# Constants and the first normalisation in one block, with plain transposes of scaled tiles and half a projection unit inside

## The chip, the cores and the metric

The kernel runs on one core of one Trainium2 chip. The metric is the device time of the program in microseconds (us), the median of the runs of a kernel. The engines are TensorE (PE, with its weight loads as PEld), VectorE (DVE), ScalarE (ACT), GpSimd (POOL) and SyncE (SP), whose queue issues every DMA here. They run side by side and wait for each other by semaphores.

## The reference

A two-layer decoder trunk on x (1, 1024, 1024) float32. Each layer is an RMS norm, one input projection, a token mixer, a gate, an output projection and a residual add. Layer 0 is a gated DeltaNet with 8 heads in chunks, layer 1 a dilated sliding-window attention with three groups of 8 heads. What matters here:

```
def rms_norm(x, g):
    y = x * lax.rsqrt(jnp.mean(x * x, axis=-1, keepdims=True) + EPS)
    return y * g
for i in range(2):
    h = rms_norm(x, norm_g[i])
    y = mixer_i(h, ...)          # proj = h @ w_in; layer 0 takes 16 columns of it as b_logit, a_logit
    x = x + y
```

In layer 0 the 16 logit columns give beta (a sigmoid) and g (the log decay of each step and head); the decays are summed along the positions before any head can use them.

## The kernel before, in words

The program is a row of blocks, and a block ends on all engines before the next begins: constants, the first norm (n0), the DeltaNet heads, the output projection (p0), the second norm (n1), the attention heads, the output projection (p1). Loads into SBUF and matmuls of a block wait for its begin.

**Constants** (lines 82 to 188). SP loads seven small tensors. POOL makes the identity and masks one after the other (line 124), PE turns the loaded rows into columns (lines 163 to 171), DVE copies them out of PSUM (lines 183 to 188), and POOL cuts the last mask behind that.

**norm_and_turn** (line 230) makes from x, 8 tiles of 128 tokens, the transposed normalised activations in two parts: g.h_hi, rounded to the matmul format fp32r, and g.h_lo, the rest. Tile t: ACT squares it with a running sum (line 270), takes Ln (272) and Exp (274), which gives 1/rms; DVE scales the identity by it into diag (301); PE multiplies 8 blocks of x by diag (289), which turns and scales at once, and each of these float32 matmuls is two passes in the trace; DVE multiplies by the gain into hf (307); ACT copies hf into h_hi (279); DVE subtracts into h_lo (313). ACT works on tile t and on the copy of tile t-2 by turns. x comes in four loads (tiles 0, 1, 2 to 4, 5 to 7; line 260), the first projection weights behind them (line 211), and these are split into parts the same way (221, 226) at the end of the stage.

**delta_heads** (line 340). PE first projects the 16 logit columns for all 1024 tokens: 2 halves of 24 matmuls of 128x512 (three_passes, line 336, in thirds of 8). ACT evacuates the halves (591), PE transposes them (713), ACT and DVE make beta and the log decay (593 to 601, 888 to 895), PE sums them with two matmuls (718, 719), ACT and DVE finish the columns (603 to 605, 900 to 905), POOL picks head 0's part (545, 548). Then comes an order written out by hand: 36 slots a head on PE, in each a third (8 matmuls) of a projection unit of the next head, and behind it the small matmuls of the current one; 3 slots make one half of a unit. The other engines follow the same slots: the evacuation of a half (658), the convolution (981, 983), the weight splits (585, 876).

SP's queue is in order: a wait in it holds all later loads.

## Time and profile before

| | us |
|---|---|
| median of 3 runs | 2462.3 (2461.72 to 2463.55) |
| profiled execution: span of the core, first to last instruction | 2456.9 |
| median minus span (start and end of the program around it) | 5.4 |
| PE, DVE, ACT, POOL busy | 2336.6, 1439.4, 1263.6, 232.5 |
| n0 ends (last h_lo), first logit matmul | 40.36, 40.67 |
| first matmul of head 0 | 58.42 |
| n1 ends (last h_lo), first attention matmul | 1219.75, 1220.07 |

The profile is of one execution; the page gives no time of its own for it beside the span. All times in the rows are from the span's start. A float32 matmul or a weight load has a modelled end, so the distance from one start to the next is the better measure of PE's pace. A granted clock of 1.00 is 2.4 GHz and 0.50 is 1.2 GHz; before its first change in the trace the clock is written as 1.00 whatever it was. "Idle before" a row is the time its engine stood still, with what ended it.

### The profile page before, as it was taken

The numbers are of one execution on the slowest core, as the hardware profiler recorded it, in microseconds if no ns is written. First come the engines' busy times: TensorE is split into PE (matmuls) and PEld (weight loads), VectorE is DVE, ScalarE is ACT, GpSimd is POOL, SyncE is SP. The second block draws the span as 40 slices with busy tenths as digits, with TensorE's granted clock in tenths as the row PEclk, the third lists the DMA queues.
The fourth block names the chain that finished last, engine by engine and source line by source line (L and its number), as shares of the span: only waits on it lengthen the run. The fifth ranks groups of instructions, "written<-read, shape, count | busy, mean of one in ns | idle before, by whom it ended". The sixth has DMA issues, their size and how long they took to land. (4 is left out here: it accounts for less than half of the span.)

```text
span 2456.9 us, 35479 instructions
## 1 busy us (share of the span) xinstructions
PE 2336.6 (95%) x11486; PEld 1941.4 (79%) x11486; DVE 1439.4 (59%) x2646; ACT 1263.6 (51%) x2564; POOL 232.5 (9%) x387
## 2 busy tenths in 40 slices
PE   6999999999999998799699999999999999999969
PEld 5778887887878786588688888888888888888757
DVE  4746666575757573676473655738284654738255
ACT  4546555565655554454554545455454545454433
POOL 1021221202020202640000000000000000000000
PEclk9999999999999998899899999999999999999979
DMA  3021222203021211688411211121121211121167
GB/s 114 28 62 49 52 53 59 74 27 84 27 72 29 71 40 33 216 278 264 178 35 36 61 40 47 33 60 35 41 63 35 60 35 47 39 56 38 18 230 267
DMA packets 280352, 189.41 MB, mean 77 GB/s; under 512 B 72173, under 2 KB 258693, under 8 KB 280229
## 3 DMA queue, kind: packets, MB, share of 16 engines
q1 hardware_dynamic: 280228, 187.88, 25.8%
q8 instruction: 64, 1.05, 0.2%
q14 instruction: 60, 0.48, 0.1%
HBM read 160.38 MB, written 27.46 MB: 76 GB/s over the span
## 5 line engine op out<-in xcount | busy, mean ns | idle before, releaser
L336 PE MATMUL b_proj<-g_h_hi,wb_w_hi 128*128 128x512 f32 x1280 | 510.7, 399 | 5.0 <-PEq L234 5.0
L336 PE MATMUL b_proj<-g_h_hi,wb_w_lo 128*128 128x512 f32 x1280 | 511.2, 399 | 0.0
L336 PE MATMUL b_proj<-g_h_lo,wb_w_hi 128*128 128x512 f32 x1280 | 510.2, 399 | 0.0
L336 PE MATMUL a_proj<-g_h_hi,wa_w_hi 128*128 128x512 f32 x784 | 324.2, 414 | 7.0 <-PEq L234 6.1
L336 PE MATMUL a_proj<-g_h_lo,wa_w_hi 128*128 128x512 f32 x784 | 323.4, 413 | 0.0
L336 PE MATMUL a_proj<-g_h_hi,wa_w_lo 128*128 128x512 f32 x784 | 317.4, 405 | 0.0
L336 PEld LDWEIGHTS b_proj<-g_h_hi,wb_w_hi 128*128 128x128 f32 x1280 | 241.4, 189 | 53.9 <-issue 5.2
L336 PEld LDWEIGHTS b_proj<-g_h_hi,wb_w_lo 128*128 128x128 f32 x1280 | 241.2, 188 | 50.0
L336 PEld LDWEIGHTS b_proj<-g_h_lo,wb_w_hi 128*128 128x128 f32 x1280 | 241.4, 189 | 49.2
L1536 ACT ACTIVATE b_acc<-b_proj,g_gains 128x512 f32<-128x512 f32 x96 | 66.1, 688 | 294.6 <-DVE b_qk L1792 208.2
L336 PEld LDWEIGHTS a_proj<-g_h_hi,wa_w_hi 128*128 128x128 f32 x784 | 149.0, 190 | 38.0 <-issue 8.7
L1689 DVE TENSOR_TENSOR wb_w_lo<-wb_raw,wb_w_hi 128x1024 fp32r<-128x1024 f32 x79 | 95.9, 1214 | 139.7 <-ACT wb_w_hi L1497 139.7
L1158 PE MATMUL p_y<-p_w_hi,p_a_hi 128*128 128x512 f32 x384 | 152.2, 396 | 26.6 <-DVE p_w_lo L1125 26.6
L336 PEld LDWEIGHTS a_proj<-g_h_lo,wa_w_hi 128*128 128x128 f32 x784 | 148.9, 190 | 30.6 <-issue 1.0
L336 PEld LDWEIGHTS a_proj<-g_h_hi,wa_w_lo 128*128 128x128 f32 x784 | 149.0, 190 | 28.7
L1158 PE MATMUL p_y<-p_w_lo,p_a_hi 128*128 128x512 f32 x384 | 151.4, 394 | 0.0
L1158 PE MATMUL p_y<-p_w_hi,p_a_lo 128*128 128x512 f32 x384 | 151.1, 394 | 0.0
L983 DVE SCALAR_TENSOR_TENSOR a_acc<-a_x_raw,a_hw,a_acc 128x512 f32<-128x512 f32 x192 | 144.3, 751 | 6.8
L1125 DVE TENSOR_TENSOR p_w_lo<-p_w_raw,p_w_hi 128x1024 fp32r<-128x1024 f32 x96 | 126.8, 1321 | 0.0
L1757 DVE TENSOR_TENSOR b_sq_lo<-b_sg,b_sq_hi 128x512 fp32r<-128x512 f32 x96 | 66.2, 689 | 84.9 <-ACT b_sq_hi L1541 84.9
L1113 ACT ACTIVATE p_a_hi<-p_a_raw 128x256 fp32r<-128x256 f32 x96 | 40.1, 418 | 145.5 <-PE p_y L1158 87.6
L1158 PEld LDWEIGHTS p_y<-p_w_hi,p_a_hi 128*128 128x128 f32 x384 | 73.3, 191 | 43.3 <-DVE p_w_lo L1125 28.0
(229 smaller groups left out, 4230.7 us busy)
## 6 DMA issues: line engine op xcount, KB each, us to landing
wb_raw<-in_b_w_in_dram SPq DMA_DIRECT2D x80, 512.0 KB, 3.9
p_w_raw<-in_a_w_out_dram SPq DMA_DIRECT2D x64, 512.0 KB, 3.9
wa_raw<-in_a_w_in_dram SPq DMA_DIRECT2D x48, 512.0 KB, 4.2
p_w_raw<-in_b_w_out_dram SPq DMA_DIRECT2D x32, 512.0 KB, 4.1
a_out<-a_og SPq DMA_DIRECT2D x64, 128.0 KB, 1.8
p_a_raw<-a_out SPq DMA_DIRECT2D x64, 128.0 KB, 4.8
a_zx<-inverse_tiles SPq DMA_DIRECT2D x16, 384.0 KB, 4.4
u_tiles<-a_u SPq DMA_DIRECT2D x8, 512.0 KB, 3.2
```

The source lines that it names most:

```text
L336: last = pe.matmul(out, w[:, k, :], a[:, k, ks], start=(n == 0), stop=(n == 23))
L983: ins = dve.scalar_tensor_tensor(acc[:, half], src, w, acc[:, half], ALU.mult, ALU.add)
L1113: act.activation(a_hi[c][:, :], a_raw[:, c, :], ACT.Copy).then_inc(high, 1)
L1125: dve.tensor_tensor(w_lo[c][:, :], w_raw[:, c, :], w_hi[c][:, :].bitcast(F32), ALU.subtract).then_inc(low, 1)
L1158: mm = pe.matmul(y[part % 2][b][:, :], a_[c][:, ts], w_[c][:, ns], start=(first and c == 0 and n == 0), stop=(last and c == RING - 1 and n ...
L1536: act.activation(acc[:, half], proj[half][:, :], ACT.Copy, scale=r.gains[:, gain:gain + 1]).then_inc(rope, 1)
L1689: dve.tensor_tensor(w_lo[slot_of(j)][:, :, :], raw[:, slot_of(j)], w_hi[slot_of(j)][:, :, :].bitcast(F32), ALU.subtract).then_inc(w_low, 1)
L1757: dve.tensor_tensor(sq_lo[:, :], sg[:, q % 2], sq_hi[:, :].bitcast(F32), ALU.subtract).then_inc(sq_low, 1)
```

## The change

There is no block of its own for the constants. They become a class whose parts are issued inside the block of the first norm stage: the small loads behind x tile 0 on SP, the masks on POOL, the turns first on PE, the rows and copies first on DVE. Their PSUM space is the second projection bank, which is now allocated ahead of the block. In both norm stages the weight row of the norm is loaded to all 128 partitions (a broadcast of 4 KB to 512 KB, between x tile 0 and tile 1), and DVE makes xs = x * (1/rms) * row in one scalar_tensor_tensor per tile; PE turns xs by plain transposes with the identity (one pass each, 8 a tile); h_hi and h_lo are made straight from PSUM. diag, hf and the gain multiply are gone, and the ring has 3 tiles instead of 4. The split of the first weights comes at tile 5 instead of at the end. In the first stage PE works off the first half unit of the logits (tokens 0 to 511) in thirds behind the transposes of tiles 5, 6 and 7. In delta_heads only the second half is left in front, and the two decay matmuls move from before the first head to its slot 2.

```diff
-def constants(nc, g, norm_g, a_norm_g, b_q_norm_g, b_k_norm_g, a_conv_w, a_log, a_dt_bias):
-
-    with ExitStack() as ctx:
...
-        ps = m.ps("ps", [P, 512])
+class Constants:
...
+    def allocate(self, ctx):
+        m = Mem(self.nc, ctx, "c")
...
+    def load(self, sp):
+        rows, landed = self.rows, self.landed
+        sp.dma_start(rows[0:16, :], self.norm_g.rearrange("l (k c) -> (l k) c", c=P)).then_inc(landed, 16)
+        sp.dma_start(rows[16:18, :], self.a_norm_g.rearrange("l (k c) -> (l k) c", c=P)).then_inc(landed, 16)
+        sp.dma_start(rows[18:21, :], self.b_q_norm_g.rearrange("l g c -> (l g) c")).then_inc(landed, 16)
+        sp.dma_start(rows[21:24, :], self.b_k_norm_g.rearrange("l g c -> (l g) c")).then_inc(landed, 16)
+
+        sp.dma_start(self.conv_rows[:, :], self.a_conv_w.rearrange("l j (c n) -> (l j c) n", n=P)).then_inc(landed, 16)
+        sp.dma_start(self.head_row[:, 0:H], self.a_log).then_inc(landed, 16)
+        sp.dma_start(self.head_row[:, H:2 * H], self.a_dt_bias).then_inc(landed, 16)
...
+    def split_high(self, act, slot):
+        act.wait_ge(self.landed[slot], 16)
+        act.activation(self.hi[slot][:, :, :], self.raw[:, slot], ACT.Copy).then_inc(self.high, 1)
+
+    def split_low(self, dve, slot):
+        dve.wait_ge(self.high, slot + 1)
+        dve.tensor_tensor(self.lo[slot][:, :, :], self.raw[:, slot], self.hi[slot][:, :, :].bitcast(F32),
+                          ALU.subtract).then_inc(self.low, 1)
+
+
+def norm_and_turn(nc, tag, g, src, norm_g, layer, weights, constants=None, logits=None):
+
+
+    RING = 3
+    EARLY = T // 2 + 1
+        gain = m.sb("gain", [P, D])
         stat = m.sb("stat", [P, T, 3])
-        diag = m.sb("diag", [P, RING, P])
-        hf = m.sb("hf", [P, RING, KD, P])
+        xs = m.sb("xs", [P, RING, D])
         turned_ps = m.ps("turned_ps", [P, RING, KD, P])
+        if constants:
+            constants.allocate(ctx)
...
             for i, (a, b) in enumerate(loads):
                 sp.dma_start(x[:, a:b, :], src[a * P:b * P, :].rearrange("(t p) n -> p t n", p=P)
                              ).then_inc(landed[i], 16)
+                if i == 0:
+                    if constants:
+                        constants.load(sp)
+                    sp.dma_start(gain[:, :], norm_g[layer:layer + 1, :].partition_broadcast(P)
+                                 ).then_inc(gain_landed, 16)
             weights.load(sp)
+
+        if constants:
+            @block.gpsimd
+            def _(pool):
+                constants.masks(pool)
...
-                if t == T:
-                    weights.split_high(act)
                 if t >= 2:
-                    act.wait_ge(gained, t - 1)
-                    act.activation(g.h_hi[:, :, tokens(t - 2)], hf[:, (t - 2) % RING], ACT.Copy).then_inc(high, 1)
+                    act.wait_ge(turned, t - 1)
+                    act.activation(g.h_hi[:, :, tokens(t - 2)], turned_ps[:, (t - 2) % RING], ACT.Copy).then_inc(high, 1)
+                if t == EARLY:
+                    weights.split_high(act, 0)
+                if t == T and weights.split_both:
+                    weights.split_high(act, 1)
 
         @block.tensor
         def _(pe):
+            if constants:
+                constants.turn(pe)
             for t in range(T):
-                pe.wait_ge(landed[load_of[t]], 16)
-                pe.wait_ge(scales, t + 1)
+                pe.wait_ge(scaled, t + 1)
                 if t >= RING:
-                    pe.wait_ge(gained, t - RING + 1)
+                    pe.wait_ge(low, t - RING + 1)
                 for k in range(KD):
-                    last = pe.matmul(turned_ps[:, t % RING, k, :], x[:, t, k * P:(k + 1) * P], diag[:, t % RING, :],
-                                     start=True, stop=True)
+                    last = pe.transpose(turned_ps[:, t % RING, k, :], xs[:, t % RING, k * P:(k + 1) * P], g.ident[:, :])
                 last.then_inc(turned, 1)
+                third = t - EARLY
+                if logits is not None and third >= 0:
+                    if third == 0:
+                        pe.wait_ge(low, TH)
+                        pe.wait_ge(weights.low, 1)
+                    three_passes(pe, logits, weights.hi[0], weights.lo[0], g.h_hi, g.h_lo, slice(0, HALF), third)

         @block.vector
         def _(dve):
+            if constants:
+                constants.make_rows(dve)
             weights.clear(dve)
+            if constants:
+                constants.keep(dve)
+            dve.wait_ge(gain_landed, 16)
             for t in range(T + 2):
                 if t < T:
                     dve.wait_ge(stats, 3 * t + 3)
                     if t >= RING:
                         dve.wait_ge(turned, t - RING + 1)
-                    dve.tensor_scalar(diag[:, t % RING, :], g.ident[:, :], stat[:, t, 2:3], None,
-                                      ALU.mult).then_inc(scales, 1)
-                if 1 <= t <= T:
-                    dve.wait_ge(turned, t)
-                    if t > RING:
-                        dve.wait_ge(low, t - RING)
-                    dve.tensor_tensor(hf[:, (t - 1) % RING], turned_ps[:, (t - 1) % RING], spread(gain, 2, P),
-                                      ALU.mult).then_inc(gained, 1)
-                if t == T + 1:
-                    weights.split_low(dve)
+                    dve.scalar_tensor_tensor(xs[:, t % RING, :], x[:, t, :], stat[:, t, 2:3], gain[:, :],
+                                             ALU.mult, ALU.mult).then_inc(scaled, 1)
                 if t >= 2:
                     dve.wait_ge(high, t - 1)
-                    dve.tensor_tensor(g.h_lo[:, :, tokens(t - 2)], hf[:, (t - 2) % RING],
+                    dve.tensor_tensor(g.h_lo[:, :, tokens(t - 2)], turned_ps[:, (t - 2) % RING],
                                       g.h_hi[:, :, tokens(t - 2)].bitcast(F32), ALU.subtract).then_inc(low, 1)
+                if t == EARLY:
+                    weights.split_low(dve, 0)
+                if t == T and weights.split_both:
+                    weights.split_low(dve, 1)
...
+SETUP_DECAYS = 2
...
-def delta_heads(nc, g, weights, o_turned):
+def delta_heads(nc, g, weights, proj, o_turned):
...
-        proj = [m_.ps(f"proj{i}", [P, HALF]) for i in range(2)]
...
+            pe.sem_inc(proj_mm, 1)
             pe.wait_ge(w_low, 1)
-            for b in range(2):
-                for third in range(3):
-                    last = three_passes(pe, proj[b][:, :], w_hi[0], w_lo[0], g.h_hi, g.h_lo,
-                                        slice(b * HALF, (b + 1) * HALF), third)
-                last.then_inc(proj_mm, 1)
+            for third in range(3):
+                last = three_passes(pe, proj[1][:, :], w_hi[0], w_lo[0], g.h_hi, g.h_lo, slice(HALF, S), third)
+            last.then_inc(proj_mm, 1)
 
             pe.wait_ge(evac, 2)
             for t in range(T):
                 last = pe.transpose(turn[:, t * 2 * H:(t + 1) * 2 * H], ba[:, t * P:(t + 1) * P],
                                     g.ident[0:2 * H, 0:2 * H])
             last.then_inc(setup, 1)
-            pe.wait_ge(setup, 12)
-            log = cols[:, C_LOG].rearrange("p t h -> p (t h)")
-            pe.matmul(turn[:, 256:256 + T * H], g.tri[:, :], log, start=True, stop=True)
-            pe.matmul(turn[:, 384:384 + T * H], g.ones[:, :], log, start=True, stop=True).then_inc(setup, 1)
+
+            def decays():
+                pe.wait_ge(setup, 12)
+                log = cols[:, C_LOG].rearrange("p t h -> p (t h)")
+                pe.matmul(turn[:, 256:256 + T * H], g.tri[:, :], log, start=True, stop=True)
+                pe.matmul(turn[:, 384:384 + T * H], g.ones[:, :], log, start=True, stop=True).then_inc(setup, 1)
...
                 for s in range(SLOTS):
+                    if m is None and s == SETUP_DECAYS:
+                        decays()
...
-        constants(nc, g, norm_g, a_norm_g, b_q_norm_g, b_k_norm_g, a_conv_w, a_log, a_dt_bias)
...
             weights = WeightSlots(nc, layer, "wa", a_w_in[0], first, True)
-            norm_and_turn(nc, "n0", g, x[0], 0, weights)
-            delta_heads(nc, g, weights, a_out)
+            proj = [Mem(nc, layer, "a").ps(f"proj{i}", [P, HALF]) for i in range(2)]
+            constants = Constants(nc, g, proj[1], norm_g, a_norm_g, b_q_norm_g, b_k_norm_g, a_conv_w, a_log, a_dt_bias)
+            norm_and_turn(nc, "n0", g, x[0], norm_g, 0, weights, constants, proj[0][:, :])
+            delta_heads(nc, g, weights, proj, a_out)
...
-            norm_and_turn(nc, "n1", g, x1, 1, weights)
+            norm_and_turn(nc, "n1", g, x1, norm_g, 1, weights)
...
```

The parts of Constants that are left out (masks, turn, make_rows, keep) hold the same instructions as the old block. Left out as well: the renamed semaphores.

## Rows read from the trace of the kernel before

**Rows 1.** First part of the page: busy time, share of the span, instructions.

```profile
PE 2336.6 (95%) x11486; PEld 1941.4 (79%) x11486; DVE 1439.4 (59%) x2646; ACT 1263.6 (51%) x2564; POOL 232.5 (9%) x387
```

**Rows 2.** Busy time by window: length, engines in order, granted clock, DMA share, GB/s.

```profile
12.00:14.00 2.00, 0.00 (x0) 0.00 (x0) 0.00 (x0) 1.59 (x5) 0.00 (x0) 1.00 1.01 412
...
42.00:44.00 2.00, 2.00 (x6) 1.52 (x5) 0.00 (x0) 0.00 (x0) 0.44 (x1) 0.50 0.30 88
...
40.67:58.42 17.75, 14.71 (x60) 11.63 (x61) 1.14 (x6) 3.73 (x10) 1.77 (x1) 0.87 0.41 118
...
70.00:600.00 530.00, 518.04 (x2613) 428.14 (x2612) 337.65 (x602) 302.52 (x626) 90.69 (x205) 1.00 0.20 52
...
1183.57:1220.07 36.50, 17.90 (x129) 16.96 (x129) 23.77 (x29) 21.96 (x43) 0.00 (x0) 0.81 0.48 173
```

**Rows 3.** Timeline, start: start, duration, engine, line, what [idle before <-releaser].

```profile
8.71 1.83 SPq L260 DMA_DIRECT2D n_x<-in_x_dram  x4
...
12.35 1.06 ACT L270 ACTIVATE n_sq<-n_x 128x1024 f32<-128x1024 f32 x1 [2.35 <-DMA n_x<-in_x_dram]
...
14.44 7.48 PE L289 MATMUL n_turned_ps<-n_diag,n_x 128*128 128x128 f32 x48 [8.99 <-DVE n_diag L301]
...
17.81 1.06 ACT L270 ACTIVATE n_sq<-n_x 128x1024 f32<-128x1024 f32 x1 [2.33 <-DMA n_x<-in_x_dram]
```

**Rows 4.** Timeline of the first norm stage in its steady part.

```profile
22.90 1.04 ACT L270 ACTIVATE n_sq<-n_x 128x1024 f32<-128x1024 f32 x1
...
24.41 1.04 ACT L279 ACTIVATE g_h_hi<-n_hf 128x1024 fp32r<-128x1024 f32 x1
...
24.95 1.22 DVE L307 TENSOR_TENSOR n_hf<-n_turned_ps,g_gains 128x1024 f32<-128x1024 f32 x1
...
25.36 1.04 ACT L270 ACTIVATE n_sq<-n_x 128x1024 f32<-128x1024 f32 x1
```

**Rows 5.** Timeline from the end of that stage to the head's slot 2, TensorE.

```profile
39.14 1.22 DVE L313 TENSOR_TENSOR g_h_lo<-n_hf,g_h_hi 128x1024 fp32r<-128x1024 f32 x1
...
40.67 0.77 PE L336 MATMUL a_proj<-g_h_hi,wa_w_hi 128*128 128x512 f32 x1 [6.13 <-PEq L234]
...
45.45 0.40 PE L336 MATMUL a_proj<-g_h_hi,wa_w_lo 128*128 128x512 f32 x1
...
53.85 0.39 PE L336 MATMUL a_proj<-g_h_hi,wa_w_lo 128*128 128x512 f32 x1
...
54.92 0.67 PE L713 MATMUL a_turn<-g_ident,a_acc 16*128 16x16 f32 x8 [0.68 <-ACT a_acc L591]
...
57.95 0.43 PE L718 MATMUL a_turn<-a_cols,g_tri 128*128 128x64 f32 x2 [2.36 <-DVE a_cols L895]
...
58.42 0.48 PE L336 MATMUL a_proj<-g_h_hi,wa_w_hi 128*128 128x512 f32 x1
...
62.62 0.40 PE L336 MATMUL a_proj<-g_h_hi,wa_w_lo 128*128 128x512 f32 x1
...
63.77 0.39 PE L336 MATMUL a_proj<-g_h_lo,wa_w_hi 128*128 128x512 f32 x1
```

**Rows 6.** DMA: landing time of line 1481's loads; issues of x up to 70 us.

```profile
DMA to landing us min/median/max: 3.4/3.9/4.2
...
n_x<-in_x_dram SPq DMA_DIRECT2D x2, 1536.0 KB, 10.0
```

**Rows 7.** Timeline of TensorE round a head's transposes; then a group of the page.

```profile
104.70 0.60 PE L814 MATMUL a_turn<-g_ident,a_acc 128*128 128x128 f32 x4
...
105.06 0.48 PE L336 MATMUL a_proj<-g_h_hi,wa_w_hi 128*128 128x512 f32 x1
...
L983 DVE SCALAR_TENSOR_TENSOR a_acc<-a_x_raw,a_hw,a_acc 128x512 f32<-128x512 f32 x192 | 144.3, 751 | 6.8
```

**Rows 8.** Timeline of the second norm stage (ScalarE) and behind it (TensorE).

```profile
1198.10 1.06 ACT L270 ACTIVATE n_sq<-n_x 128x1024 f32<-128x1024 f32 x1 [2.31 <-DMA n_x<-x]
...
1220.07 0.77 PE L336 MATMUL b_proj<-g_h_hi,wb_w_hi 128*128 128x512 f32 x1 [5.00 <-PEq L234]
```

182 lines of the change are left out of this document (83 added, 99 removed).

## The prediction

> **What bounds the kernel now.** I read the page's busy shares first: TensorE (PE) is busy 95% of a span of 2456.9 us, VectorE (DVE) and ScalarE (ACT) 59% and 51% [rows 1]. So a change pays only where PE stands still or runs at its lower clock, and the next view to read is the busy time by stretch. In the 17.75 us after the first norm stage PE is busy 14.71 us at a mean clock of 0.87; in the second norm stage it is busy 17.90 us of 36.50 [rows 2]. These edges are what the change touches. Everything between them is dense PE work with nothing in it changed, so I take it that it only slides: what is won before the first head is won at the end.
>
> The timeline of the start shows the first edge. The block of constants comes first and x is loaded only behind it, at 8.71; its first tile is squared at 12.35 (3.64 us later), and ACT begins tile 2 at 17.81, when the third load has landed [rows 3]. From there the stage runs in a fixed beat: ACT squares a tile, takes Ln and Exp, copies an older tile into h_hi, and squares the next, 22.90 to 25.36, 2.46 us a tile with no gap; DVE is as full, with diag, the gain multiply (1.22) and h_lo (1.22) [rows 4, 5]. PE has room: a tile's sixteen passes take it 2.02 us. The stage ends with the last h_lo, 39.14 + 1.22 = 40.36, and PE starts the projection of the head logits at 40.67 [rows 5].
>
> That projection is 48 matmuls. Up to 45.45 they start every 0.43 us (11 of them), then every 0.233 us (the last at 53.85) [rows 5]. The windows give the slow part a clock of 0.50, that is 1.2 GHz [rows 2], after PE had stood idle for 6.13 us; the fast part has 2.4 GHz. Then come the small transposes (54.92), an idle time of 2.36 us while ACT and DVE make the decays, two small matmuls at 57.95, and the first head's first matmul at 58.42. It is slow again: 11 matmuls up to 62.62 take 4.20 us where 11 x 0.233 = 2.56 would do. The 17th, which begins slot 2, starts at 63.77 [rows 5]. I use this event as the mark: what happens up to it is changed, from it on the program is the same.
>
> **The change, part by part.** (1) One block for constants and norm. x tile 0 is issued at 0.83 instead of 8.71. Seven small loads and the broadcast norm row stand before the rest of x on SP's queue. The small ones took 0.83 to about 3.4 to issue; behind tile 0 they end near 3.7, so the broadcast goes out at 3.7 and x tile 1 at 4.2. A broadcast of this very shape (one row to 128 partitions, 512 KB) lands 3.4 to 4.2 us after issue [rows 6], here at about 7.4. Once it flows, x comes in at 412 GB/s [rows 2], 1.3 us for half a megabyte and 3.8 for the three tiles of a 1536 KB load, which before landed some 10 us after its issue because it queued behind the others [rows 6]. Queued behind the broadcast, tile 1 lands near 8.7 and tiles 2 to 4 at about 12.5. I take 12.6 for the start of tile 2 on ACT, 5.2 us earlier than 17.81: 7.9 us of earlier issue, less 1.4 for the small loads' issue and 1.3 for half a megabyte more. Bounds 11.5 and 14.5 (the broadcast overlapping fully, or the small loads delaying it). The constants themselves are covered: PE's turns and DVE's five copies, done at 6.2 before, are done at about 7, and DVE's first scaling waits for the broadcast, 7.4, in any case; POOL's masks are beside it.
>
> (2) The new tile. DVE loses diag and the PSUM multiply and gains one scalar_tensor_tensor of 128x1024. There is none in the trace; the 128x512 one takes 751 ns [rows 7], a tensor_tensor of 1024 takes 1.22 [rows 4], so it lies between 1.2 and 1.5; I take 1.25, since most of an instruction's time is per element. DVE then needs 2.4 a tile, ACT still 0.95 + 0.22 + 0.24 + 0.10 + 0.95 = 2.46. ACT's h_hi copy now reads PSUM; a 128x512 copy from PSUM takes 0.59, no more than SBUF ones, so nothing is added. The beat stays 2.46: the removed DVE work is worth nothing by itself. PE's sixteen passes become eight transposes: four take 0.36 us at the full clock in a head (104.70 to 105.06) [rows 7], so 0.72 and some 0.25 to drain; at the half clock twice that, at most 0.23 each as the first tiles' passes show (48 in 7.48 us, 1.9 us over the later rate) [rows 3]. Either is under 2.46.
>
> (3) Where this puts the tail. From 12.6: tile 5's square starts at 12.6 + 3 x 2.46 = 20.0; its h_hi companion ends at 22.5; the weight split of slot 0 on ACT 23.45, on DVE 25.1 (weights landed near 17). So the first third of the logits' half unit starts at 25.15, right behind tile 5's transposes. Now PE is in series with the tiles: third 0, tile 6, third 1, tile 7, third 2. A third is 8 matmuls: 3.4 us slow, 1.87 fast. I assume the clock rises during or just after third 0, as it did after 2.5 to 4.8 us of PE work at 14.44, 40.67 and 58.42: third 0 ends at 28.55, tile 6 at 30.0, third 1 at 31.9, tile 7 at 32.8, third 2 at 34.7. h_hi of tile 7 ends at 33.9, its h_lo at 35.1. Block end 35.1, next matmul 35.4 (the 0.31 us step of [rows 5]).
>
> (4) After the stage. Only 24 logit matmuls are left. PE has been idle under 1 us before them, so I take them at 0.233: 5.6 us. Last result to transposes 0.83 + 0.55 as before, then slots 0 and 1 of the head (16 x 0.23 = 3.7) at once, which more than covers the 2.36 us that the decays need, then the two decay matmuls 0.47. Mark at 35.4 + 5.6 + 1.38 + 3.7 + 0.47 = 46.55 against 63.77: 17.2 us earlier. By parts: 5.3 for the stage, 5.6 for the half unit that moved into it, 2.4 idle, 2.2 and 1.65 for the two slow starts of the clock. A cost hides here: the decays' last exponentials, the head's taps and the weight split of unit 1 were done before slot 2 began and now come after it. ACT is through them 2.45 us after the mark, DVE 3.7, so the first convolution begins about 0.9 us later than it did; the second one waits for its own half's evacuation, so this is absorbed, and PE's next weights are due only 4 slots (7.4 us) after the mark. If that cover were gone, the price would be this 0.9 us once.
>
> (5) The second norm stage has the same new tiles and no constants. The broadcast stands between tile 0 and tile 1 there, and tile 2 on ACT already waits for its load (1198.10) [rows 8], so the beat starts 1.3 us later. The weight split moved from the tail into it (0.95 on ACT, which is now full to the end: last Exp at 1199.4 + 5 x 2.46 + 0.94 + 1.6 = 1214.25), but the tail is shorter: scaling 1.25, transposes 1.0 to 1.8, h_hi 1.05, h_lo 1.2. End 1218.9 to 1219.7 against 1219.75. PE's start there was slow before too (1220.07, idle 5.00 us) [rows 8]. I take zero; bounds -1 and +2 (the clock's slow start longer by half, or the broadcast costing more).
>
> The Trainium skill, "TensorE: Matmul & The Clock Gate", Part 4: PE-mode transpose, speaks against the change: the full clock does not engage for transposes, which do not count as PE work the way matmuls do. The trace of before has 128-wide transposes only in fours between dense matmuls at the full clock [rows 7], so it neither confirms nor denies it. By it, taking matmuls out of the norm stage takes the warming out too, which is the first rival below.
>
> **Sum.** Own time of the profiled execution: span 2456.9; the median of the runs is 2462.3, 5.4 more lies around the span and is not touched. 2456.9 - 17.2 + 0 = 2439.7 span, 2445.1 us.
>
> **Rivals.** A, slow tail: transposes and short thirds leave PE at 1.2 GHz to the end of the stage and through the half unit. Third 0 to 28.55, tile 6 30.0, third 1 33.4, tile 7 34.9, third 2 38.3; block end 38.7, matmuls from 39.0, 24 of them at the pace of [rows 5] 7.8: mark 52.35, 11.4 saved, 2450.9. For it: five tiles of transposes at 40% of the beat or less before third 0. Against: third 0 alone is 3.4 us of dense matmuls, about what raised the clock at 58.42. B, fast tail: the clock is at 2.4 GHz from tile 2 on, as it was with the matmuls. Third 0 ends at 27.0, last h_lo at 32.9, mark 44.35: 19.4 saved, 2442.9. C, the saving does not survive: the first head's chain (setup, convolution, block inverses and their round trip through memory) sets the pace of the first heads, not PE, and it starts hardly earlier than PE's cover shrinks, or the new loads crowd the start; under 4.9 us left, 2457.4 to 2467. Against: from 70 to 600 PE is busy 518.04 of 530 us [rows 2]. D, slower: DVE's wait for the broadcast stands at the head of its queue in both stages; behind it is every scaling, transposes and h_hi. It decides against the change if the 128 reads of one row take over 17 us more together than the 4 us of [rows 6], say 10 us each: 2462.3 + 3 = 2465. Against: the row of that shape, measured eight times.
>
> **How the numbers follow.** Forecast 0.57, A 0.20, B 0.15, C 0.05, D 0.03. Prediction 2445.1. The range takes in B with a second stage at -1, 2442, and A with +2, 2453. Under 0.2% (4.9 us) a measurement of this kernel can hardly be told from no change, so: faster 0.92, same 0.05, slower 0.03.
>
> **What would show it.** Right: x issued at 0.8; tile 2's square near 12.6; a beat of 2.46 on ACT with DVE below it; 8 transposes a tile; third 0 at 25; a projection start near 35.4 with PE idle under 1 us before; no idle between the logits' transposes and the head; the mark near 46.5, and the same distance from mark to end except for the second norm stage. Wrong: a clock of 0.50 between 30 and 45 (A); tile 2's square after 14.5; gaps in PE in the first head that were not there (C); a second stage over 2 us longer.

## The result, and the profile after

Median 2449.4 us (2446.8 to 2450.2, four runs) against 2462.0 (2458.5 to 2463.6, four runs): ratio 0.9946, interval 0.9932 to 0.996. The change saves 12.6 us; 17.2 were forecast. The time lies inside the range, 4.3 us above the forecast and close to rival A's 2450.9, though mostly not for A's reason. The profiled execution has a span of 2445.1 and took 2446.8. From the page after, its first part:

```profile
PE 2324.5 (95%) x11358; PEld 1927.6 (79%) x11358; DVE 1438.4 (59%) x2630; ACT 1262.9 (52%) x2564; POOL 230.8 (9%) x387
```

TensorE's busy time fell by 12.1 us against [rows 1] and the span by 11.8. No share tells what happened; the edges do. The timeline of after, from the start to the first third of the half unit (start, duration, engine, line, what [idle before <-releaser]):

```profile
0.83 0.39 SPq L269 DMA_DIRECT2D n_x<-in_x_dram  x1
...
3.73 0.35 SPq L274 DMA_DIRECT2D n_gain<-in_norm_g_dram  x1
...
8.12 1.28 DVE L333 SCALAR_TENSOR_TENSOR n_xs<-n_x,n_stat,n_gain 128x1024 f32<-128x1024 f32 x1 [0.90 <-DMA n_gain<-in_norm_g_dram]
...
13.32 1.06 ACT L289 ACTIVATE n_sq<-n_x 128x1024 f32<-128x1024 f32 x1 [2.26 <-DMA n_x<-in_x_dram]
...
18.16 1.05 ACT L289 ACTIVATE n_sq<-n_x 128x1024 f32<-128x1024 f32 x1
...
18.73 1.97 PE L311 MATMUL n_turned_ps<-g_ident,n_xs 128*128 128x128 f32 x8 [0.45 <-DVE n_xs L333]
...
20.58 1.05 ACT L289 ACTIVATE n_sq<-n_x 128x1024 f32<-128x1024 f32 x1
21.14 1.64 PE L311 MATMUL n_turned_ps<-g_ident,n_xs 128*128 128x128 f32 x8 [0.45 <-DVE n_xs L333]
...
23.56 1.09 PE L311 MATMUL n_turned_ps<-g_ident,n_xs 128*128 128x128 f32 x8 [0.78 <-DVE n_xs L333]
...
25.92 0.76 PE L365 MATMUL a_proj<-g_h_hi,wa_w_hi 128*128 128x512 f32 x1 [1.26 <-DVE wa_w_lo L233]
...
29.04 0.43 PE L365 MATMUL a_proj<-g_h_lo,wa_w_hi 128*128 128x512 f32 x1
...
30.10 0.47 PE L365 MATMUL a_proj<-g_h_hi,wa_w_lo 128*128 128x512 f32 x1
...
35.94 0.47 PE L365 MATMUL a_proj<-g_h_hi,wa_w_hi 128*128 128x512 f32 x1 [1.05 <-PEq L242]
...
42.37 0.66 PE L740 MATMUL a_turn<-g_ident,a_acc 16*128 16x16 f32 x8 [0.68 <-ACT a_acc L619]
...
46.75 0.33 PE L747 MATMUL a_turn<-a_cols,g_tri 128*128 128x64 f32 x2
...
47.11 0.48 PE L365 MATMUL a_proj<-g_h_lo,wa_w_hi 128*128 128x512 f32 x1
```

x is issued at 0.83, tile 2 is squared at 13.32 in place of 17.81 ([rows 3]), and the beat is 2.42 us (18.16 to 20.58). The projection behind the stage starts at 35.94 (40.67 before), at full pace; nothing waits between the small transposes and the head (2.36 us in [rows 5]); the mark, last row, is at 47.11 against 63.77.

The windows of after round third 0 and in the second norm stage (length, PE, PEld, DVE, ACT, POOL, granted clock, DMA share, GB/s):

```profile
24.00:26.00 2.00, 0.74 (x7) 0.53 (x5) 2.00 (x3) 1.94 (x6) 0.00 (x0) 0.93 0.00 0
26.00:28.00 2.00, 2.00 (x5) 1.61 (x6) 2.00 (x2) 1.94 (x6) 0.00 (x0) 0.50 0.00 0
28.00:30.00 2.00, 2.00 (x11) 1.62 (x11) 2.00 (x3) 0.88 (x1) 0.00 (x0) 0.72 0.00 0
...
1190.00:1193.00 3.00, 2.55 (x12) 2.15 (x12) 3.00 (x3) 2.88 (x9) 0.00 (x0) 0.50 0.09 23
1193.00:1195.00 2.00, 1.21 (x11) 0.97 (x10) 2.00 (x3) 2.00 (x3) 0.00 (x0) 0.98 0.00 0
...
1197.00:1203.00 6.00, 3.94 (x16) 3.14 (x16) 5.35 (x5) 4.48 (x8) 0.00 (x0) 0.50 0.00 0
1205.00:1209.00 4.00, 4.00 (x10) 3.13 (x11) 1.22 (x1) 2.04 (x2) 0.00 (x0) 0.50 0.45 131
```

The last four windows are the second norm stage and the attention matmuls behind it. The timeline of after there:

```profile
1172.87 0.32 SPq L269 DMA_DIRECT2D n_x<-x  x1
...
1177.70 1.06 ACT L289 ACTIVATE n_sq<-n_x 128x1024 f32<-128x1024 f32 x1 [3.54 <-DMA n_x<-x]
...
1184.10 1.06 ACT L289 ACTIVATE n_sq<-n_x 128x1024 f32<-128x1024 f32 x1 [2.22 <-DMA n_x<-x]
...
1203.20 1.23 DVE L337 TENSOR_TENSOR g_h_lo<-n_turned_ps,g_h_hi 128x1024 fp32r<-128x1024 f32 x1 [0.85 <-ACT g_h_hi L296]
...
1204.74 0.76 PE L365 MATMUL b_proj<-g_h_hi,wb_w_hi 128*128 128x512 f32 x1 [2.64 <-PEq L242]
...
1210.00 0.47 PE L365 MATMUL b_proj<-g_h_hi,wb_w_hi 128*128 128x512 f32 x1
```

Twelve times the next matmul starts 0.43 us or more behind the last before the pace becomes 0.23 (1210.00); before the change it was six times. So the first edge came out as forecast and the second did not.

The distances between the same events in several profiles, in us (the names of the other kernels are explained below), show where the 17.2 went. "First layer out" is the output projection of layer 0, "tile 2's square" is ScalarE's first work on tile 2 of the second norm stage, and slow matmuls are the first ones of the attention projection whose successor starts over 0.4 us later:

| stretch | before | before_again | after | after_again | n1_old | gain_early | warm |
|---|---|---|---|---|---|---|---|
| start to mark | 63.77 | 63.75 | 47.11 | 47.45 | 47.44 | 45.59 | 45.63 |
| mark to last projection matmul of layer 0 (the heads) | 869.72 | 868.48 | 872.36 | 871.54 | 872.31 | 873.99 | 873.14 |
| mark to last first-layer-out matmul | 1119.30 | 1119.21 | 1119.65 | 1120.63 | 1119.87 | 1123.56 | 1120.93 |
| last first-layer-out matmul to tile 2's square | 15.03 | 15.19 | 17.34 | 17.22 | 16.03 | 15.94 | 17.24 |
| tile 2's square to first attention matmul | 21.96 | 21.92 | 20.64 | 20.64 | 21.37 | 20.54 | 19.77 |
| slow matmuls there | 6 | 7 | 12 | 11 | 6 | 8 | 0 |
| first to last attention projection matmul (with its slow start) | 1104.70 | 1106.43 | 1106.80 | 1106.66 | 1105.49 | 1106.10 | 1103.88 |
| last of these to first matmul of the second output projection | 36.76 | 37.84 | 37.37 | 37.28 | 35.30 | 35.27 | 37.72 |
| last matmul to end | 6.13 | 6.14 | 7.07 | 7.07 | 6.12 | 7.07 | 6.13 |

In spans: 16.66 won at the mark; 1.0 lost in the second stage (+2.31 to tile 2, -1.32 behind it); 1.2 lost to the longer slow start (six more slow matmuls at 0.20 each); 0.94 lost at the last store; 11.8 left, so 1.7 are in the long stretches between. The two profiles of the unchanged kernel differ by 1.7 and 1.1 in two such stretches, and by 3.2 in span: the net 1.7 can't be told from the spread of one execution.

Inside it is something that can. The heads of layer 0, whose code behind the mark is the same, took 868.5 to 869.7 us in the three profiles with the old order in front of them (before, before_again and one_block, explained below) and 871.3 to 876.1 in all eleven others; both kinds were profiled on two of the chips, and the gap is there on each. In after they are 2.6 us longer, and a stretch behind them, up to the end of the output projection, that came out 2.3 us shorter hides it. PE's waits in the heads, first in before (63.77 to 933.4), then in after (47.11 to 919.5), with total, times and longest in us:

```profile
PE a_first L858 <- DMA a_zx<-inverse_tiles: 4.2, 4, 3.2
...
PE a_first L889 <- DMA a_zx<-inverse_tiles: 6.7, 6, 3.6
```

2.5 us more wait for the block inverses that come back through memory, which is the chain that rival C named. What in the change lengthens it was not tested; decays_front and logits_back, which undo a part each, have it too (872.3 and 876.1).

### The profile page after: what moved, and what is told of

Same layout as the page of the kernel before. It is cut to its first block and busy times, and to the rows that moved or that the text cites. A ratio compares the mean times of both kernels' runs of the same rounds, so it can differ in the third digit from the quotient of the medians.

```text
span 2445.1 us, 35190 instructions
## 1 busy us (share of the span) xinstructions
PE 2324.5 (95%) x11358; PEld 1927.6 (79%) x11358; DVE 1438.4 (59%) x2630; ACT 1262.9 (52%) x2564; POOL 230.8 (9%) x387
```

## The experiments

Each is an edit of the changed kernel unless it says so; kernels in one group ran on one chip with the same runs of before, so medians of different groups are best compared by their ratio to before.

**The two kernels again (before_again, after_again).**

> The kernel before, unchanged, to learn how far one execution differs from another. In the profile of the changed kernel the head's slot 2 began 16.7 us earlier than before, but the span was only 11.8 us shorter; 4.9 us went between slot 2 and the end. Theory 1 (the loss is the change's own, at the second norm stage): this second profile of before repeats the first within 0.5 us in every stage, above all 929.7 us from slot 2 (63.77) to the last transposed output of the heads (993.50) and 1104.7 us from the first to the last attention projection matmul. Theory 2 (the loss is the spread of single executions): these stages differ by 1 to 2 us between the two profiles of the same code.

> The changed kernel, unchanged, timed in five rounds. Theory 1: median 12 to 13 us below before again, and in the profile the second norm stage with the slow start of the attention behind it costs the same 2 to 3 us more than before. Theory 2: a saving of 15 to 17 us in these rounds, the first result having been a low draw.

Measured: before_again 2462.5 us, ratio 1.0003 (0.9994 to 1.0012); after_again 2448.3, 0.9945 (0.9931 to 0.9958). The saving is 13.8 and 12.6 in two comparisons. before_again's profile differs from before's by 1.7 us in the attention projection, so its Theory 2 (the spread of single executions) holds for the long stretches; after_again's Theory 1 holds for the median and for the second stage and the end, whose distances repeat to 0.2 us in these pairs.

**Second norm stage as before (n1_old).** The first stage is the changed one, the second runs the old method.

```diff
-            norm_and_turn(nc, "n1", g, x1, norm_g, 1, weights)
+            norm_and_turn_old(nc, "n1", g, x1, 1, weights)
```

> The changed kernel with the second norm stage as it was before (matmuls with the scaled identity, gain multiply, no broadcast); the first stage stays changed. In the changed kernel the 13 first attention matmuls ran at the half clock (7 before), and the third x load of that stage was squared 6.4 us after the first (5.7 before). Theory 1: 2 to 3 us faster than the changed kernel (slow start back to 7 matmuls, 1.2 us; last tile's turn 0.9; load 0.7 to 1.3), the first attention matmul about 1 us earlier after the last matmul of the output projection, 37.0 us instead of 38.0. Theory 2 and the forecast of zero for this stage: no difference beyond 1 us.

Measured: 2446.4 us, 0.9941 (0.9928 to 0.9955), 1.9 better than after_again in the medians. From last layer-out matmul to first attention matmul it takes 37.40 against 37.86, it has 6 slow matmuls in place of 11, and its last store lands 0.95 sooner. These are the three losses of the table, taken back in part: 0.5, 1.0 and 0.95. The intervals overlap; the profile's distances carry the reading, and they are one execution's. In this pair the new method costs about 1.5 us in the second stage and is worth nothing there. But the old method does not always do better: one_block, which has it too, takes 38.30 us for the same stretch and has 12 slow matmuls behind it, with the same idle time of 5.00 us as before. Timeline of one_block:

```profile
1215.28 0.77 PE L362 MATMUL b_proj<-g_h_hi,wb_w_hi 128*128 128x512 f32 x1 [5.00 <-PEq L243]
...
1220.53 0.44 PE L362 MATMUL b_proj<-g_h_hi,wb_w_hi 128*128 128x512 f32 x1
```

There the granted clock was full from 1193.3 and fell at 1213.8, 1.5 us before the projection; in before it fell at 1219.6, 0.5 us before it. So the slow start was 6, 7, 6 and 12 matmuls with the old method, and 11 to 13 in six profiles with the new one (8 in gain_early).

**PE kept at its full clock (warm).** Matmuls of a constant, whose results nobody uses, fill PE's gaps in both stages.

```diff
+            def keep_warm(n):
+                for _ in range(n):
+                    pe.matmul(idle[:, :], g.ones_r[:, :], warm[:, :], start=True, stop=True)
...
+            keep_warm(10 if constants else 16)
             for t in range(T):
...
+                if t < 5 if constants else t < 7:
+                    keep_warm(3)
+                elif not constants:
+                    keep_warm(8)
```

> The changed kernel with matmuls of constants added on TensorE in its idle time in both norm stages (10 and 16 before the first tile, 3 behind each of tiles 0 to 4 and 0 to 6, 8 behind tile 7 of the second stage); their results go to a spare bank and are not used. Theory 1 (plain transposes do not keep TensorE at the full clock, and this costs at the stage ends): the windows show 1.00 from the first tiles on, third 0 of the half unit takes 1.9 us instead of 3.4, a tile's turn 1.1 instead of 2.0, the attention starts with no slow matmul; first logit matmul behind the stage near 34.3 instead of 35.9, in all 4 to 6 us faster than the changed kernel. Theory 2 (the clock is not what costs): the same time within 1 us.

Measured: 2444.5 us, 0.9931 (0.9917 to 0.9944), 3.8 below after_again; the intervals overlap a little. Timeline of warm, TensorE:

```profile
23.65 1.09 PE L322 MATMUL n_turned_ps<-g_ident,n_xs 128*128 128x128 f32 x8 [0.63 <-DVE n_xs L349]
26.01 0.47 PE L381 MATMUL a_proj<-g_h_hi,wa_w_hi 128*128 128x512 f32 x1 [1.26 <-DVE wa_w_lo L233]
...
34.46 0.47 PE L381 MATMUL a_proj<-g_h_hi,wa_w_hi 128*128 128x512 f32 x1 [0.96 <-PEq L242]
...
1203.57 0.47 PE L381 MATMUL b_proj<-g_h_hi,wb_w_hi 128*128 128x512 f32 x1 [0.79 <-PEq L242]
```

Third 0 runs at full pace from its first matmul, the stage ends 1.5 us sooner (34.46), and the attention projection has no slow start. So the clock was worth 1.5 to 1.8 us at the first edge and, at the second, 0.87 in the stage's tail (20.64 to 19.77) and some 2.3 in the start behind it (11 or 12 x 0.2). The last store lands 0.95 sooner here too; it did so in n1_old as well, where the clock is not held. That is 5.8 against a difference of 5.3 in the spans and 3.8 in the medians.

**The second stage turned by matmuls (n1_matmul_turn).** The data and the order stay; each transpose becomes a float32 matmul with the identity, which is two passes, so PE also gets twice the passes.

```diff
-                    last = pe.transpose(turned_ps[:, t % RING, k, :], xs[:, t % RING, k * P:(k + 1) * P], g.ident[:, :])
+                    if constants:
+                        last = pe.transpose(turned_ps[:, t % RING, k, :], xs[:, t % RING, k * P:(k + 1) * P], g.ident[:, :])
+                    else:
+                        last = pe.matmul(turned_ps[:, t % RING, k, :], xs[:, t % RING, k * P:(k + 1) * P], g.ident[:, :],
+                                         start=True, stop=True)
```

(constants are given in the first stage alone)

> The changed kernel with the turns of the second stage made by float32 matmuls with the identity (two passes, 16 a tile) instead of plain transposes; all else equal. Theory (matmul passes raise the clock, transposes hardly do): the windows of that stage show 1.00 from the second or third tile on as before the change, a tile's turn 2.0 us, the attention starts with 7 or fewer slow matmuls instead of 13 (1.2 us less), the stage's own length stays. Median 0.5 to 1.5 us below the changed kernel. Rival: the clock follows the share of time in which TensorE is busy, whatever it does; then the same share of passes at 2.0 us in a beat of 2.41 gives the same half clock, and nothing changes.

Measured: 2446.2 us, 0.9932 (0.9919 to 0.9944; its highest run 2451.7), beside 0.9945 (0.9931 to 0.9958) for the changed kernel: the intervals overlap, and the profiled execution is the slowest of the six, so again the reading rests on the stage in one profile. Windows and timeline of n1_matmul_turn:

```profile
1190.00:1192.00 2.00, 2.00 (x12) 2.00 (x12) 0.77 (x1) 1.94 (x5) 0.00 (x0) 0.54 1.01 406
1192.00:1194.00 2.00, 2.00 (x18) 1.90 (x18) 2.00 (x3) 1.94 (x6) 0.00 (x0) 1.00 1.11 321
```

```profile
1203.28 2.05 PE L314 MATMUL n_turned_ps<-g_ident,n_xs 128*128 128x128 f32 x16 [1.41 <-DVE n_xs L337]
...
1210.30 0.47 PE L369 MATMUL b_proj<-g_h_hi,wb_w_hi 128*128 128x512 f32 x1 [2.64 <-PEq L242]
```

Sixteen passes a tile at 2.05 us in place of eight transposes at 1.97, so the stage is as long (20.72 from tile 2). But the clock rises at 1191.8, in the second tile, and stays, and the projection starts at full pace behind the same idle time of 2.64 us. In the changed kernel, behind the same idle time, the clock was already low. So in this pair what PE did in the stage, and not the idle gap behind it, decided the twelve slow matmuls. Whether the kind of instruction counts or its amount is not shown: before the clock rises a tile's sixteen passes keep PE busy for 3.6 us, without a gap, and eight transposes for 1.97 of 2.42 us. The forecast's rival (the share of busy time decides) is not excluded by this test, and pad_b below speaks for it.

**Parts undone: the decays in front (decays_front), the half unit behind the stage (logits_back).**

```diff
+            decays()
+
             def body(m, n, p):
...
-                    if m is None and s == SETUP_DECAYS:
-                        decays()
```

> The changed kernel with the two decay matmuls back in front of the first head, as before. Theory (each part pays at its own place and keeps it): TensorE idles again 2.3 us after the logits' transposes, and the clock falls for about 3.4 us of the first head's matmuls (1.65 us lost); the head's slot 2 begins 3.5 to 4.2 us later than in the changed kernel (47.1 to 47.5), and the median is 3 to 4.5 us above it, near 2452. Rival (what is won at the start is given back in the heads): slot 2 is later by the same, but the span and the median are not, within 1.5 us.

```diff
-            norm_and_turn(nc, "n0", g, x[0], norm_g, 0, weights, constants, proj[0][:, :])
+            norm_and_turn(nc, "n0", g, x[0], norm_g, 0, weights, constants)
```

(and all 48 logit matmuls behind the stage)

> The changed kernel without the half unit in the norm stage: both halves of the logits behind it, the decays still at slot 2. The stage should end 1.5 to 2.4 us earlier (no thirds between the transposes), the logits take 24 matmuls more and start at the half clock: first matmul behind the stage near 34, second half's end near 47.5 against 41.5. Theory: slot 2 of the head 5.5 to 6 us later than in the changed kernel, median near 2454. Rival (the half unit only moved, since it holds up the tiles): under 3 us.

Measured: decays_front 2453.8, 0.9965 (0.9952 to 0.9978), 5.5 above the changed kernel's 2448.3; logits_back 2454.8, 0.9967 (0.9955 to 0.998), 6.5 above. Their intervals meet its own (0.9931 to 0.9958) at the edge only. Timeline of decays_front, and of logits_back:

```profile
41.47 0.66 PE L740 MATMUL a_turn<-g_ident,a_acc 16*128 16x16 f32 x8 [0.68 <-ACT a_acc L619]
44.50 0.43 PE L747 MATMUL a_turn<-a_cols,g_tri 128*128 128x64 f32 x2 [2.36 <-DVE a_cols L926]
```

```profile
34.21 0.77 PE L365 MATMUL a_proj<-g_h_hi,wa_w_hi 128*128 128x512 f32 x1 [2.83 <-PEq L242]
48.74 0.67 PE L741 MATMUL a_turn<-g_ident,a_acc 16*128 16x16 f32 x8 [0.68 <-ACT a_acc L619]
```

The idle 2.36 us of [rows 5] is back to the hundredth, with the slow start behind it: mark 50.31, though its stage had happened to end 0.9 earlier (transposes 41.47 against 42.37), so 4.1 for the order alone. Without the thirds the stage ends 1.7 sooner (34.21) and the small transposes come 6.4 later (48.74): the 24 matmuls cost the stage 1.7 and save 8.1 behind it, which is their 5.6 and a slow start. The mark is at 53.50.

**Second norm row loaded early (gain_early).** The row of layer 1 is fetched in the output projection of layer 0.

```diff
-        gain = m.sb("gain", [P, D])
+        gain = m.sb("gain", [P, D]) if constants else g.gain1
...
+            if rope_tables:
+                sp.dma_start(rope_tables.g.gain1[:, :], rope_tables.norm_g[1:2, :].partition_broadcast(P)
+                             ).then_inc(rope_tables.g.gain1_landed, 16)
```

> The changed kernel with the second stage's weight row loaded at the end of the output projection before it, into a tile of its own. Theory (the 512 KB in the queue between tile 0 and tile 1 costs 1.3 to 2 us there): from the last matmul of the first output projection to the square of tile 2 15.1 to 15.5 us instead of 17.2 to 17.3, and the first attention matmul 1.3 to 2 us earlier; median 1 to 2 us below the changed kernel. Rival (those 2 us are the DMA's spread or the stores' landing): the distance stays above 16.5.

Measured: 2445.6 us, 0.9932 (0.9919 to 0.9945), 2.7 below the changed kernel's 2448.3, with overlapping intervals. The distance to tile 2 is 15.94 for 17.34, and 16.03 in warm_gain_early, which has the early row too; all eight profiles with the broadcast in the queue have 17.15 to 17.37. So the broadcast between x tile 0 and the rest costs 1.1 to 1.4, as step (5) had it. Its first edge was quick too (mark 45.59) though that code is the same. Timeline of gain_early, to be held against its three rows in after (21.14, 23.56, 25.92):

```profile
21.18 1.97 PE L311 MATMUL n_turned_ps<-g_ident,n_xs 128*128 128x128 f32 x8 [0.45 <-DVE n_xs L333]
23.60 1.83 PE L311 MATMUL n_turned_ps<-g_ident,n_xs 128*128 128x128 f32 x8 [0.45 <-DVE n_xs L333]
25.96 0.47 PE L365 MATMUL a_proj<-g_h_hi,wa_w_hi 128*128 128x512 f32 x1 [0.53 <-DVE wa_w_lo L233]
```

In after the full pace came on tile 4 (1.64), held for tile 5 (1.09) and was gone when third 0 began; here it came as tile 5 ended, and third 0 had all of it. So of this profile's gain 1.5 is the clock's phase at the first edge, and 1.3 is what the edit explains; how the 2.7 in the medians divides is not shown.

**Before with the constants' block alone (one_block).** An edit of the kernel before: one block, x issued first, a ring of 3 tiles, but the old scaling and the old turn by diag, and no broadcast.

```diff
-        constants(nc, g, norm_g, a_norm_g, b_q_norm_g, b_k_norm_g, a_conv_w, a_log, a_dt_bias)
...
+            proj = [Mem(nc, layer, "a").ps(f"proj{i}", [P, HALF]) for i in range(2)]
+            constants = Constants(nc, g, proj[1], norm_g, a_norm_g, b_q_norm_g, b_k_norm_g, a_conv_w, a_log, a_dt_bias)
+            norm_and_turn(nc, "n0", g, x[0], 0, weights, constants)
```

> The kernel before with one part of the change alone: the constants inside the block of the first norm stage (small loads behind x tile 0, masks, turns and copies there), the old tile method, ring of 3 tiles. Theory (the stage's gain is the earlier load, less 1.3 us for the broadcast that the whole change adds): tile 2 squared near 12.0 instead of 17.81, first logit matmul near 34.5 to 35 instead of 40.67, and the same 5.5 to 6 us at the end; median near 2456.5. Rival (the plain transposes and the fused scaling carry part of the stage's gain): under 4 us.

Measured: 2458.5 us, 0.9969 (0.996 to 0.9979), 8.1 less than the before of its comparison (2466.5; 5.2 to 9.9 by the interval, where 5.5 to 6 were expected). Timeline of one_block, TensorE:

```profile
34.40 0.77 PE L362 MATMUL a_proj<-g_h_hi,wa_w_hi 128*128 128x512 f32 x1 [6.13 <-PEq L243]
...
48.73 0.66 PE L738 MATMUL a_turn<-g_ident,a_acc 16*128 16x16 f32 x8 [0.68 <-ACT a_acc L616]
51.76 0.43 PE L743 MATMUL a_turn<-a_cols,g_tri 128*128 128x64 f32 x2 [2.37 <-DVE a_cols L920]
```

34.40 for 40.67: the early issue of x is worth 6.3 us; up to the mark the rest is as before (idle 6.13, idle 2.37), and the mark moves by 6.2. Tile 2 is squared at 11.42 here and at 13.32 in after, which also waits for the broadcast. Of the 16.66 at the mark the block gives 6.2, the half unit 6.4 (logits_back) and the later decays 4.1 (decays_front); by this sum the new tile, with its broadcast, is left with about nothing.

**Warm and early row together (warm_gain_early).**

> The changed kernel with both additions: matmuls of constants in TensorE's idle time of both norm stages, and the second stage's weight row loaded behind the output projection. If the two add up: 5 to 6 us below the changed kernel, median 2442 to 2443.5, faster than all others. Rival: the first attention matmul is bound by the beat of ScalarE, and the earlier load is worth nothing once the clock is up: 2444.5.

Measured: 2447.2 us where before takes 2466.5: 0.9922 (0.9909 to 0.9935), 19.3 us saved, the lowest ratio of all. The median itself missed the forecast 2442 to 2443.5, since this chip is some 4 us slower with before too. Against the change itself (0.9945, 0.9931 to 0.9958) the ratio is 0.23% of 2466 lower, 5.7 us, as forecast, but its interval meets that one at the edge and overlaps those of warm and gain_early. From the last layer-out matmul to the first attention matmul it takes 35.80 us, 37.01 in warm and 36.47 in gain_early, so the early row still pays 1.2 with the clock up, against the rival. The added matmuls did not hold the clock without fail: it fell for 3.4 us at 18.2 and again at 1188.9.

**A few tiny matmuls in the first block (pad_a 8, pad_b 20),** to move the later code in memory without touching the second stage.

```diff
                 constants.turn(pe)
+                pe.wait_ge(constants.kept, 5)
+                for _ in range(8):
+                    pe.matmul(constants.ps[:, 0:1], g.ones_r[:, :].bitcast(F32), g.ones[:, 0:1], start=True, stop=True)
```

> The changed kernel with 8 matmuls of one column added on TensorE in its idle time before the first tile (32 instructions with their weight loads; their result is not used), to move TensorE's code against the blocks in which code is fetched. In the changed kernel the last store landed 3.66 us after its issue in both executions (2.7 in the kernel before, n1_old and warm), with one packet of an instruction queue in that stretch, and the second stage's first x load 4.8 us after issue (3.2), with one or two such packets. Theory (fetched code shares the DMA engines with these loads, and where it falls hangs on the code's length): with the code shifted, at least one of the two landings goes back to 2.7 and 3.2, and its stretch has no packet of that queue. Rival (the landing times have another cause): both stay at 3.66 and 4.8 whatever the code.

> As pad_a with 20 such matmuls (80 instructions). Theory: a landing is long in the runs whose stretch holds a packet of an instruction queue and short in the others, in this run as in the rest. Rival: no such relation.

Measured, one execution each: 2449.8 and 2454.1 us. Against this chip's 2466.5 for before that is 16.7 and 12.5 less, with no interval. In both, x tile 0 of the second stage lands 3.2 us after its issue as it did before the change (4.8 in after), while tile 2 is no earlier (17.25 and 17.15 from the last layer-out matmul). The last store is as late as in after (3.67). pad_b has a price of its own; timeline of pad_b:

```profile
7.46 8.69 PE L308 MATMUL a_proj<-g_ones,g_ones_r 128*128 128x1 f32 x40 [0.81 <-DVE g_pair_mask L197]
16.01 4.56 PE L314 MATMUL n_turned_ps<-g_ident,n_xs 128*128 128x128 f32 x24
21.90 1.09 PE L314 MATMUL n_turned_ps<-g_ident,n_xs 128*128 128x128 f32 x8 [1.33 <-DVE n_xs L336]
...
26.74 1.97 PE L314 MATMUL n_turned_ps<-g_ident,n_xs 128*128 128x128 f32 x8 [1.33 <-DVE n_xs L336]
```

Twenty one-column matmuls took 8.69 us and held the transposes back to 16.01, so its mark is at 50.67. It shows something else by accident: of its 24 transposes in a row the first 16 start 0.21 us apart and the last ones 0.11 (24 in 4.56 us; eight at half pace take 1.97). The clock rose at 19.6, in the midst of transposes without a gap, much as it rose at 18.07 in before in the midst of 48 matmul passes without a gap from 14.44 on; it held for two tiles with gaps of 1.33 (1.09 each), and fell at 26.4. The one-column matmuls had kept PE busy before, so this is not a test of transposes alone.

## Why the prediction was right, and where it failed

(1) One block. Right in kind: tile 2's square was forecast at 12.6 and came at 13.32. The broadcast reached DVE at 8.12, not 7.4: 4.4 us from its issue, just over the range of [rows 6]. one_block confirms the term (6.2 at the mark).

(2) The tile. The scalar_tensor_tensor of 1024: 1.28 (taken 1.25). Beat 2.42 (taken 2.46). Eight transposes: 1.09 at the full clock (taken 0.97) and 1.97 at half. The removed DVE work is worth nothing in the beat, as forecast. Behind tile 2 the new method is 2.1 us shorter (from its square to the next matmul 20.83 in logits_back, 22.98 in one_block), which is about what its later tile 2 costs.

(3) The tail. Third 0 at 25.92 (25.15), third 1 at 30.10 (30.0), end of the stage 35.37 (35.1), next matmul 35.94 (35.4). Of the 0.7 lost in (1) the beat and the tail won back a part; 0.5 was left at the next matmul. I had the clock rise in third 0, "after 2.5 to 4.8 us of PE work". The trace of before has 3.6 at least (14.44 to the rise at 18.07; 4.7 and 4.0 at the others), so no row has the 2.5; in after the clock rose on third 0's last matmuls, at 29.1. The Trainium skill, "TensorE: Matmul & The Clock Gate", Part 4: PE-mode transpose, says that the full clock does not engage for transposes. These traces bear out its direction and not its letter. Direction: the first tiles ran at half pace in every execution with transposes and no other matmuls among them, and n1_matmul_turn's second stage, which has matmuls in place of the transposes (and twice the passes), had the full clock from its second tile and kept it. Letter: in eight of the nine first stages of that kind the pace doubled between 19.6 and 25.6 us, on transposes alone; in six of them it fell again 3.4 to 6.8 us later, with gaps between the tiles. Where it came early (after, after_again, n1_old, pad_a: tile 5 in 1.09) it was gone before third 0 or within its first two matmuls, and most of its matmuls were slow; where it came at the end of tile 5 (gain_early, decays_front) third 0 was at full pace. The same code thus has its mark between 45.6 and 47.5. Rival B's fast third 0 came in two executions, A's slow half unit in none: third 0 brings the clock up by its end, and A needed it to stay down through thirds 1 and 2.

(4) Behind the stage. 24 matmuls at 0.23, transposes, the head at once: mark 47.11 for 46.55. decays_front and logits_back put each part back: 4.1 and 6.4 us at the mark, where the forecast's terms are 4.05 (2.4 idle and 1.65 slow start) and 6.1 (5.6 and 2.2, less the 1.7 that the thirds cost the stage). The hidden price was there too: the first convolution began 3.55 us after the mark, 0.8 later than before (taken 0.9), but the small matmul that next depends on the convolution's chain (L831, L800 before) starts 12.9 us after the mark where it started 12.8 after it, with PE full up to it: absorbed there. But the heads as a whole took 2.6 us longer in after, see above; decays_front, whose first convolution begins as early as before (2.77 us after the mark), has the longer heads too, so this price is not their cause.

(5) The second norm stage is the step that failed. I put it at zero, from +1.3 for the broadcast against a shorter tail. Both were right (+1.3 by gain_early; the part behind tile 2 is 1.32 shorter). Three things made it dearer. First, 2.3 us and not 1.3 are lost up to tile 2. The other 1.0 is neither the new tile's nor the broadcast's: n1_old and one_block, with the old method and no broadcast, take 16.03 and 16.92 to tile 2, and gain_early 15.94, where before takes 15.03 and 15.19. Nor is it x tile 0's landing, 1.6 us later in after: in the pads and in warm it is early and the distance is 17.15 to 17.25 all the same. What it is stays open. Second, the clock's slow start was listed as a bound only ("longer by half") and is what happened, 12 matmuls for 6, +1.2; one_block shows 12 with the old method as well, so a part of this may be the clock's phase. Third, the last store, 1200 us behind the last edit, lands 0.94 later. The stage and its slow start together are 2.1 us dearer, at the +2 that was my bound, and with the store it is 3.1. I had argued rival A for the first stage alone, where a third of matmuls comes to the rescue; the second has transposes and nothing else, so a low clock should have been charged there first. The premise that everything behind the mark only slides failed too: the heads did not (+2.6 in after), though in that profile the shorter stretch behind them made up for it.

Sum. I took 5.4 us to lie around the span. after's profiled execution took 2446.8 with a span of 2445.1, so 1.7 lie around it; the other 3.7 were a profiled execution quicker than the median. That doesn't change a difference, but a forecast made on one profile carries it. Forecast 17.2, found 12.6 in medians: 0.5 at the mark, 1.0 in the second stage, 1.2 in its slow start, 0.9 at the end, by the profiles, and 1.0 that can't be told from the spread. That the median landed in the range is partly luck: the range reached to 2453 for rival A's slow tail, which did not come, and losses of another kind used that room.

Rival C did not come in its size, but in part: the heads, mark to last projection matmul, are 2.6 us longer in after, 2.5 of it more waiting for the block inverses. From the mark to the last layer-out matmul after lost 0.35 net, after_again 1.4, and the profiles of the four kernels in the group of gain_early 3.3 to 6.5; no profile of before was taken on that chip, so how much of this is the chip's is not shown. Rival D did not come: the broadcast takes 4.4 us in the first stage and 5.7, behind x tile 0, in the second, not 10.

## What to carry to other kernels

An edge of a kernel, where the engine that sets the time stands still, can be read off the timeline event by event, and a sum of terms from its rows came within 0.6 us of a 16.7 us saving. Charge every use of a shared helper, not only the one for which the edit was made: the second stage had no constants to hide and no matmuls between its transposes, so it got the price alone. Look at a long stretch that only slides with its own distance in both profiles, and at the parts of it: a net change of 0.35 us here hid 2.6 one way and 2.3 the other. And what an idle engine is fed matters to the work behind it: where the transposes of the second stage end in dense matmuls, matmuls that compute the same thing left the stage as long and had no slow start, in the one profile taken.

## What the runs showed of the hardware

**Landing times and instruction fetches.** The DMA view of a stretch also lists queues that move instructions. For x tile 0 of the second stage in after, 1172.87 to 1177.68:

```profile
q1 hardware_dynamic: 268, 1.02, 72.7%
q8 instruction: 1, 0.02, 1.3%
q14 instruction: 1, 0.01, 0.4%
```

In the six profiles with a q8 packet in that stretch the tile landed 4.3 to 4.9 us after issue; in the eight without one, 3.18 to 3.28. For the last store: 2.71 to 2.73 in the six profiles without an instruction packet, 3.66 to 3.67 in the eight with one from q14. Data and size are the same in all. A q14 packet alone does not tell: the stretch of x tile 0 has one in all fourteen, early and late. Eight tiny matmuls some 1160 us earlier took the q8 packet away and left the last store's. So an edit far from a load, which changes only the length of PE's code in between, went with a landing 1.0 to 1.6 us earlier or later. That the packet delays the landing is a reading of a coincidence in 14 profiles, not shown by an edit that removes the packet alone.

**The clock column at the start.** In after it reads 1.00 up to its first entry, the rise at 22.3 us, while eight transposes take 1.97 (18.73); in the second stage it reads 0.50 with the same 1.97, and 0.98 with 1.09. Before its first change the pace of the instructions, not the column, tells the clock.

**The clock rose in stages with transposes alone, and did not stay with gaps between them.** In the second stage of after eight transposes of a tile take 1.97 us at a granted clock of 0.50, 1.09 at 0.98 (1193 to 1195), and 1.97 again. In warm, with three matmuls behind each tile, they take 1.09 from the second tile of the first stage on and throughout the second.

**Tiny matmuls aren't cheap.** One-column float32 matmuls took 0.22 us a pass (8.69 for 40 in pad_b), as long as one of the slow 128-column transposes behind them (0.21).
